# The last mixer of a two-block fp32 transformer on one core: gate and upper projection in halves, the first item's softmax beside them, a convolution of three steps a tick at the end

## What is computed

```python
u = h @ w_in
q, kc, vc, ks, vs, kw, vw, gt, cf = jnp.split(u, offs, axis=-1)
# queries and keys are normalised and rotated; 8 heads of 64, 2 groups of keys
kc = rms_norm(compress_blocks(kc_tok, cmp_pos[0], cmp_w1[0], cmp_w2[0]), k_norm[2])
vc = compress_blocks(v_cmp, cmp_pos[1], cmp_w1[1], cmp_w2[1])   # gelu(flat @ w1) @ w2
# per head: compressed attention, attention to selected blocks, attention in a window
out = gate0 * o_cmp + gate1 * o_slc + gate2 * o_win
a, b = jnp.split(cf, 2, axis=-1)
z = a * jax.nn.sigmoid(b)
z = causal_dwconv(z, conf_dw) + conf_dw_b                       # 32 taps
z = jax.nn.silu(layer_norm_2(z, conf_ln_g, conf_ln_b))
return jnp.concatenate([o_nsa, z], axis=-1) @ w_out
```

## Time and profile before

| | |
|---|---|
| Median of three runs | 2248.85 us |
| The profiled execution | 2248.29 us |
| Its span in the profile | 2246.5 us |
| PE busy | 2219.8 us, 99% of the span |
| DVE, ACT, POOL busy | 1629.2, 1196.7, 126.6 us |
| Mean granted clock of PE | 0.998 of full speed |
| DMA, mean over the span | 182 GB/s |

### The profile page before, as it was taken

How to read it: one execution, slowest core, us unless ns; L and a number is a source line. 1 busy time by engine, 2 the same in 40 slices (tenths; PEclk the granted TensorE clock), 3 DMA queues, 4 the chain that set the end, 5 groups by cost and what they waited for, 6 DMA issues and landing times.

```text
span 2246.5 us, 34599 instructions
## 1 busy us (share of the span) xinstructions
PE 2219.8 (99%) x14127; PEld 1906.0 (85%) x14127; DVE 1629.2 (73%) x2508; ACT 1196.7 (53%) x1896; POOL 126.6 (6%) x185
## 2 busy tenths in 40 slices
PE   8999999999999999999999999999999999989999
PEld 7888899878888888888898778888888888867887
DVE  5777768868676876768668777676877678666776
ACT  5555446645555545555356544555444655556653
POOL 2100010120000000000100110000000000420000
PEclk9999999999999999999999999999999999999999
DMA  7765564445556556656554446555655655643654
GB/s 237 226 190 195 189 218 123 139 153 188 191 187 193 187 185 210 191 189 196 194 180 141 135 155 210 192 186 174 206 173 173 212 188 189 199 132 117 198 176 150
DMA packets 284207, 408.17 MB, mean 182 GB/s; under 512 B 13828, under 2 KB 171072, under 8 KB 283792
## 3 DMA queue, kind: packets, MB, share of 16 engines
q1 hardware_dynamic: 276096, 380.84, 52.6%
q0 software_dynamic: 7808, 25.04, 3.7%
q10 hardware_dynamic: 144, 0.07, 0.0%
HBM read 403.98 MB, written 1.91 MB: 181 GB/s over the span
## 4 chain that ended last, share of the span: by engine, by line
PE 90%; DVE 6%; ACT 3%; DMA 1%; issue 1%; POOL 0%; SPq 0%; DVEq 0%; ACTq 0%
PE PS L575 24%; PE PS L506 12%; PE PS L513 12%; PE PS L507 12%; PE PS L574 11%; PE PS L472 2%; PE PS L473 2%; PE PS L474 2%; PE PS L577 2%; DVE WL L1391 1%; PE PS L558 1%; PE PS L557 1%; PE PS L556 1%; PE PS L492 1%; DVE QX L1698 1%
## 5 line engine op out<-in xcount | busy, mean ns | idle before, releaser
L1391 DVE TENSOR_TENSOR WL<-RW,WH 128x1024 fp32r<-128x1024 f32 (+2 forms) x678 | 803.9, 1219 | 173.2 <-ACT WH L1007 169.3
L575 PE MATMUL PS<-XT,WH 128*128 128x512 f32 x2368 | 808.0, 394 | 0.0
L1007 ACT ACTIVATE WH<-RW 128x1024 fp32r<-128x1024 f32 (+2 forms) x678 | 679.5, 1042 | 188.8 <-DMA RW<-in_w_in 39.8
L574 PE MATMUL PS<-XT,WL 128*128 128x256 f32 x2072 | 581.2, 280 | 0.0
L575 PEld LDWEIGHTS PS<-XT,WH 128*128 128x128 f32 x2368 | 425.4, 188 | 75.8
L574 PEld LDWEIGHTS PS<-XT,WL 128*128 128x128 f32 x2072 | 389.9, 188 | 13.4
L506 PE MATMUL PS<-WH,XT 128*128 128x512 f32 (+2 forms) x592 | 229.8, 392 | 1.3 <-DVE WL L1391 0.8
L507 PE MATMUL PS<-WL,XT 128*128 128x512 f32 (+2 forms) x592 | 222.2, 379 | 0.0
L506 PE MATMUL PS<-WH,HTH 128*128 128x512 f32 x488 | 192.8, 395 | 0.0
L507 PE MATMUL PS<-WL,HTH 128*128 128x512 f32 x488 | 191.6, 393 | 0.0
L513 PE MATMUL PS<-WH,XT 128*128 128x512 f32 (+2 forms) x592 | 174.1, 380 | 0.0
(11 more groups left out here) (519 smaller groups left out, 3281.6 us busy)
## 6 DMA issues: line engine op xcount, KB each, us to landing
RW<-in_w_ff_in SPq DMA_DIRECT2D x252, 512.0 KB, 4.4
RW<-in_w_ff_out SPq DMA_DIRECT2D x128, 512.0 KB, 4.3
RW<-in_w_in SPq DMA_DIRECT2D x56, 512.0 KB, 4.6
RW<-in_w_gate SPq DMA_DIRECT2D x48, 512.0 KB, 4.0
RW<-in_ffn_gate SPq DMA_DIRECT2D x44, 512.0 KB, 4.4
RW<-in_ffn_up SPq DMA_DIRECT2D x44, 512.0 KB, 4.4
RW<-in_ffn_down SPq DMA_DIRECT2D x44, 512.0 KB, 4.5
RW<-in_w_out SPq DMA_DIRECT2D x16, 512.0 KB, 5.2
```

The lines of the kernel that those rows point to most:

```text
L574: self.e.matmul(k.PS[:, b.n, 0:T], wl, k.XTH[:, kt, :], start=False, stop=False)
L575: ins = self.e.matmul(k.PS[:, b.n, :], wh, k.XT[:, kt, :], start=kt == 0, stop=kt == 7)
L1007: self.e.activation(u.hi_out, raw, ACT.Copy).then_inc(*self.s["hi"].up(u.n))
L1391: self.e.tensor_tensor(u.lo_out, raw, u.hi_out.bitcast(F), ALU.subtract).then_inc(*self.s["lo"].up(u.n))
```

## The change

It does five things.

- The keys' rotation for t = 0 is issued after the fourth step of the queries' rows and that for t = 1, with the doubled copy of the keys, after the eighth; before, both stood ahead of these rows. The two turns of paired rows move from the seventh and eighth step to the sixth and seventh.
- The gate is projected in two halves (columns 1816 and 2072 on), and so the walk is gate half 0, upper half 0, then in the tick loop gate half 1 and upper half 1. The loads of this stretch were four units of 512 KB and eight of 256 KB, and are sixteen of 256 KB: the same bytes.
- The list `beside` has eight places with the same kinds of work, and now item 0's scores behind the sixth step, its maximum behind the seventh (in one call with the compressed keys' norm and the eviction of gate half 0), and its exponentials and scale after the eighth. Item 0 has four more yields ahead of its product with the values, and each item one yield less between exponentials and scale and one at its end.
- The four copies of the compressed values (`cmp_values`, VCB) come after the norm of the compressed keys.
- From the sixteenth tick on the convolution has three steps a tick in place of two.

In the changed file the lines of `cmp_out` and after have moved by four (L1391 is L1395, L1636 is L1640, L2088 is L2092, L2112 is L2116).

```diff
@@ -1298,17 +1298,21 @@
     def cmp_out(self, b):
         k = self.k
         self.wait_ge("mm", b.full)
-        self.wait_ge("odd_g", "vcb0")
-        for i in range(4):
-            r = slice(32 * i, 32 * i + 32)
-            self.e.activation(k.VCB[r, i], k.PS[r, b.n, 128:256].rearrange("p (g d) -> p g d", g=2),
-                              ACT.Copy).then_inc(*self.s["odd_a"].up(("vcb", i)))
         kr = k.PS[:, b.n, 0:128].rearrange("p (g d) -> p g d", g=2)
         ms = k.MS[:, 24:26]
         self.e.activation(k.KCN[:, :, 0, :], kr, ACT.Square).then_inc(*self.s["odd_a"].up("ksq"))
         self.wait_ge("odd_v", "ksum")
         self.wait_ge("const_v", "eps")
         self.e.activation(ms, ms, ACT.Sqrt, bias=k.eps[1e-6], scale=1.0 / 64).then_inc(*self.s["odd_a"].up("kroot"))
+
+    def cmp_values(self, b):
+        k = self.k
+        self.wait_ge("odd_v", "kn0")
+        self.wait_ge("odd_g", "vcb0")
+        for i in range(4):
+            r = slice(32 * i, 32 * i + 32)
+            self.e.activation(k.VCB[r, i], k.PS[r, b.n, 128:256].rearrange("p (g d) -> p g d", g=2),
+                              ACT.Copy).then_inc(*self.s["odd_a"].up(("vcb", i)))
 
     def cmp_keys(self, b):
         k = self.k
...
-        for t in range(2):
-            e.rotate("k", t, 8, 12)
         e.windows()
         for _ in range(2):
             load_w1()
-        e.keys_double()
+
+        def rotated_keys(t):
+            e.rotate("k", t, 8, 12)
+            if t:
+                e.keys_double()
...
+        compressed_out = []
+
         def compressed_rows():
             b = self.bank()
             e.cmp_out(b)
             e.cmp_norm(b)
             e.prepare(ACT.Tanh)
-            self.drop(b, ("odd_a", "ksq"), ("odd_v", "kn0"))
+            compressed_out.append(b)
...
         bks = [self.bank(), self.bank()]
-        beside = [e.nothing] * 6 + [lambda: paired(0), lambda: paired(1)]
+        beside = [e.nothing, e.nothing, e.nothing, lambda: rotated_keys(0), e.nothing, lambda: paired(0),
+                  lambda: paired(1), lambda: rotated_keys(1)]
         for _ in self.rows(w, 8, 0, [(0, 512, bks)], self.x):
...
-        bks = [self.bank() for _ in range(4)]
-        beside = [lambda: e.rotate("q", 0, 0, 8), lambda: e.rotate("q", 1, 0, 8), hidden,
-                  lambda: (e.clear_vcb(), features("k", 0), features("k", 1)), hidden_turn, lambda: features("q", 0),
-                  compressed_rows, e.nothing]
-        for _ in self.cols(w, 1816, 4, bks, self.x, steps=2):
-            beside.pop(0)()
-        features("q", 1)
-        compressed_keys()
-        for j in range(4):
-            e.odd_gate(j, bks[j])
-            self.drop(bks[j], ("odd_a", ("sg", j)))
-        for n in range(2):
-            e.conv_weights(n)
-
         turned, done = set(), {0: [], 1: []}
-        later = {"q1": False}
-
-        def compressed():
-            bks = [self.bank(), self.bank()]
-            e.cmp_scores(bks)
-            for b in bks:
-                self.drop(b, ("odd_v", "cs"))
-            yield
-            yield
-            e.cmp_probs()
-            yield
-            while not later["q1"]:
-                yield
-            b = self.bank()
-            e.cmp_probs_turn(b)
-            self.drop(b, ("odd_a", "ptc"))
-            yield
...
         def item(n, t, hs):
 
-            while any(ROOM[m] == ROOM[n] and m not in turned for m in range(n)) or ROOM[n] and not later["q1"]:
+            while any(ROOM[m] == ROOM[n] and m not in turned for m in range(n)) :
                 yield
...
                 self.drop(bb[i], ("att_a", (A.id, "exp")))
             if n == 7:
                 e.prepare(ACT.Sqrt)
+            e.odd_scale(I)
             yield
-            e.odd_scale(I)
             yield
             while n >= 2 and ("out", n - 2) not in turned:
...
             yield
             yield
+            if n == 0:
+                yield
+                yield
+                yield
+                yield
             b = self.bank()
             e.odd_out(I, b)
             turned.add(("out", n))
...
+            yield
+
+        items = [item(n, t, hs) for n, (t, hs) in enumerate(
+            [(0, [0, 2]), (0, [4, 6]), (0, [1, 3]), (0, [5, 7]), (1, [0, 1]), (1, [2, 3]), (1, [4, 5]), (1, [6, 7])])]
+
+        gates, ups = [self.bank(), self.bank()], [self.bank(), self.bank()]
+
+        def gated(half, bks):
+            for j in range(2):
+                e.odd_gate(2 * half + j, bks[j])
+                self.drop(bks[j], ("odd_a", ("sg", 2 * half + j)))
+
+        def raised(half, bks):
+            for j in range(2):
+                e.odd_up(2 * half + j, bks[j])
+                self.drop(bks[j], ("odd_v", ("zc", 2 * half + j)))
+            e.conv_out(half)
+            e.conv_shift(half)
+
+        def cleared():
+            e.clear_vcb()
+            for n in range(2):
+                e.conv_weights(n)
+            features("k", 0)
+            features("k", 1)
+
+        beside = [lambda: e.rotate("q", 0, 0, 8), lambda: e.rotate("q", 1, 0, 8), hidden, cleared,
+                  lambda: (hidden_turn(), features("q", 0)), lambda: next(items[0]),
+                  lambda: (compressed_rows(), gated(0, gates), next(items[0])), e.nothing]
+        for c0, bks in ((1816, gates), (1304, ups)):
+            for _ in self.cols(w, c0, 2, bks, self.x):
+                beside.pop(0)()
+        next(items[0])
+        raised(0, ups)
+        features("q", 1)
+        compressed_keys()
+        e.cmp_values(*compressed_out)
+        self.drop(*compressed_out, ("odd_a", ("vcb", 3)), ("odd_v", "kn0"))
...
+        def compressed():
+            bks = [self.bank(), self.bank()]
+            e.cmp_scores(bks)
+            for b in bks:
+                self.drop(b, ("odd_v", "cs"))
+            yield
+            yield
+            e.cmp_probs()
+            yield
+            yield
+            b = self.bank()
+            e.cmp_probs_turn(b)
+            self.drop(b, ("odd_a", "ptc"))
             yield
...
         def upper():
 
-            for half in range(2):
+            for c0, end in ((1816 + 256, gated), (1304 + 256, raised)):
                 bks = [self.bank(), self.bank()]
-                for n, _ in enumerate(self.cols(w, 1304 + 256 * half, 2, bks, self.x)):
+                for n, _ in enumerate(self.cols(w, c0, 2, bks, self.x)):
                     if n == 3:
-                        for j in range(2):
-                            e.odd_up(2 * half + j, bks[j])
-                            self.drop(bks[j], ("odd_v", ("zc", 2 * half + j)))
-                        e.conv_out(half)
-                        e.conv_shift(half)
+                        end(1, bks)
                     yield
 
         y = self.out_odd(Operand(k.OTH, k.OTL, lambda kt, t: done[t] if kt < 4 else [("turn_lo", ("conf", t))]))
-        items = [item(n, t, hs) for n, (t, hs) in enumerate(
-            [(0, [0, 2]), (0, [4, 6]), (0, [1, 3]), (0, [5, 7]), (1, [0, 1]), (1, [2, 3]), (1, [4, 5]), (1, [6, 7])])]
-        gens = [(1, items[0]), (1, compressed()), (2, items[1]), (2, items[2]), (3, items[3]), (3, items[4]), (3, items[5]),
+        gens = [(0, items[0]), (1, compressed()), (0, items[1]), (2, items[2]), (3, items[3]), (3, items[4]), (3, items[5]),
                 (3, items[6]), (3, items[7])]
...
             ticks += 1
-            if ticks == 4:
-                later["q1"] = True
             live = [g for g in live if next(g, self) is not self]
             if up:
                 if next(up, self) is self:
                     up = None
             elif conv:
-                for _ in range(2):
+                for _ in range(2 if ticks < 16 else 3):
                     if conv and next(conv, self) is self:
                         conv = None
                         live += [conformer(0), conformer(1)]
```

More of the change, by code:

```diff
@@ L459 @@
     conv_out = conv_shift = conv_weights = conv_taps4 = conv_sum = paired = odd_q = cmp_hidden = cmp_turn = cmp_out = features = keys_double = nothing
-    cmp_norm = cmp_keys = cmp_scores = cmp_probs = cmp_probs_turn = odd_scores = odd_max = odd_scale = odd_turn = odd_out = nothing
+    cmp_norm = cmp_values = cmp_keys = cmp_scores = cmp_probs = cmp_probs_turn = odd_scores = odd_max = odd_scale = odd_turn = odd_out = nothing
     conf_turn = conf_norm = conf_back = nothing
```

## The result

The changed kernel takes 2251.49 us (median of 20 runs, 2247.76 to 2254.35), the kernel before 2247.85 (median of 20, 2245.26 to 2253.01). The ratio is 1.0016 with a 95% interval of 1.0010 to 1.0023: it is slower by 3.6 us, less than the 4.5 us that the prediction called a difference, but outside of the interval and not the 0.0 that was forecast. The profiled execution took 2249.53 us with a span of 2247.7; 16 of the 20 runs were slower than it, so the trace shows the change in one of its faster executions.

A forecast was written before the change was run, and what follows sets the result against it. TensorE bounds the kernel, busy 2219.8 of 2246.5 us, with 11.7 us of idle and low clock to win. Transposes 6.2 earlier, +3.65 late wait, +1.7 and +0.85 clock sum to 0.0: 2248.8 us, range 2244.5 to 2251.9.

The forecast's parts named there:

- (a): Keys rotated later: PE's wait before the first gate step goes from 1.53 us to 0, hidden layer begins 2.1 earlier.
- (b): Gate and upper weights loaded as sixteen units of 256 KB: same bytes, four loads more, priced at 0.
- Rival C: Narrow weight units land late and column steps wait: 6.6 us slower, 2255.4 us; chance 0.07.
- (c): First softmax, waits before L897, the second gate half and L943: 2.8 us in place of 1.38 + 2.15.
- (d): Compressed probabilities: waits before L920 and the second item's L943, taken 1.5 us; before, 1.87 before L920.
- (e): Convolution at three steps a tick: idle of the second stretch taken 1.2 us, in place of 2.50.
- (f): Last item's split stands behind the conformer on ACT and DVE: new PE wait in the output projection, +3.65 us.
- (g): Low clock behind new idles: +1.7 us behind the late wait, +0.85 (0 or 1.7) behind the item's wait.
- Rival B: The late wait before the output projection's second-half rows is hidden, the split being ready in time: 2243.5 us; chance 0.14.
- D: Clock falls at all three stalls (item 0, compressed probabilities, the end): +2.55, 2251.4 us; chance 0.13.

The follow-up runs named there:

- step ahead: Split run plus one more column step of gate half 1 ahead of the first item's turn, against the kernel before: 2241.18 us, ratio 0.9973.
- split run: Changed kernel with the last item's output split directly after its product, ahead of the conformer's activation; against the kernel before: 2246.52 us, ratio 0.9988.
- loads moved: Changed kernel with POOL's loads of the second half of Z behind its third group of diagonal copies; against the kernel before: 2248.77 us, ratio 0.9997.
- best version: Changed kernel with last split first, POOL's Z loads later and one column step ahead of the first item's turn; against the kernel before: 2239.80 us, ratio 0.9964.

## Why the prediction was wrong, step by step

- **(a), (b)** held in the changed kernel's profile. The first gate step doesn't wait, the hidden layer is 2.1 us earlier, and PE waits for no weight unit whose load is late. In three of the edited kernels, whose order is the same up to there, that step waited 0.26 to 0.63 for its cast, so the 1.53 isn't always won whole. Rival C is refuted: the kernel got slower by another mechanism. The figure of the Trainium skill ("DMA: Bandwidth & Descriptors", "Anatomy of one DMA") beside rival C is for DMAs that GpSimd issues, and these are SP's; the 2.7 us of the trace agree with it all the same.
- **(c)** held, a little too high: 0.25 + 0.33 + 1.85 = 2.4 us, 2.8 taken, at the three places named.
- **(d)** was too high: 1.5 taken, 0.1 measured. With the low clock behind item 0 one could say that slow matmuls hid it, but in the runs with the step ahead, whose low clock is 3.4 us, it was 0.33 at most as well. The chain of the compressed probabilities has more cover than I gave it.
- **(e) failed, and this is the first of the two steps that made the forecast wrong.** Taken 1.2, measured 2.0 in the profile of the changed kernel and 3.75 in that of the split run, with a fall of the clock besides. Without the meeting it is 0.4 + 0.7 = 1.1, so the propagation along the queues was right. What it lacked is that an instruction's duration, read where no POOL operation lay beside it, isn't its duration beside POOL. I wrote that POOL's copies would be the first to run short; PE never waited for one in this profile, DVE did. Price: 2.7 us in the changed kernel by the medians with the loads moved.
- **(f)** held: 3.61 for 3.65. **Its clock in (g)** was mis-sized: taken 3.4 us at half, 1.7; measured 6.8 us, some 2.7 by the instructions' starts in the profile; in two edited kernels it was 3.4 us. Medians put the whole place at 5.0 and 5.4, against 3.65 + 1.7 = 5.35 predicted.
- **(g) for item 0 failed in size, the second step.** The forecast gave back 2.1 for the old low clock and took 0.85, a mean of 0 and 1.7, for the new one: 1.25 us won. The 1.85 us stall was followed by 10.2 us of low clock, in others of the runs by 6.8 or 3.4 behind the same stall. Against the 6.8 us of the earlier trace rows it cost 1.5 more: 1.5 us lost. That is 2.75 off. (By the busy times above the old low clock had cost nearer 2.9 than 2.1; as the difference alone counts, that changes nothing here.)
- **The sum.** Forecast 0.0, found +3.6: +2.7 from the meeting, which is in no term, +2.75 from item 0's low clock, -1.8 from (c) and (d), which were taken too high, and nearly nothing from the rest. The parts come from medians and from single profiles, so that they meet 3.6 this well is in part luck. Rival B is refuted (the late wait was there). D's 2251.4 is nearest, by luck: it has no meeting, and it prices a fall behind the compressed probabilities, where no stall was left. The changed kernel's profiled execution is 2 us faster than its median; that the meeting was shorter in it than in most (PE's wait of 1.60; five profiles of other kernels with the eight copies at this place have 1.53 to 3.36) is likely, but no slower execution of this kernel was profiled.
- **Slips that decide nothing.** The low end of the range is worked out as 2244.5 and used as 2244.0; rival C's 7.0 + 0.6 + 0.68 is 8.3 and not 8.2.

What stays open is what sets the length and the beginning of a low clock. The same stall of 1.86 us in the same order was followed by 10.2, 6.8 and 3.4 us in different executions; the longer ones began 0.7 to 1.5 us after the turn of item 0, the one of 3.4 us began 3.4 us after it.

## What to carry to other kernels

Moving one group of work ahead of another in a program that is written once for all engines also moves it on queues where nobody looks: follow the last user of each queue to the end of the stage. When two engines can block each other, a duration from a trace holds only for the neighbours it had there; look which of the other engine's rows will lie beside it after the move. The length of such a meeting, and that of a low clock, differed between profiles of the same order: compare several of them before you trust one. The spread of the runs alone doesn't tell of a meeting: the twenty of the kernel before, whose product took 0.22 in its profile, spread over 7.8 us.

## What the runs showed of the hardware

- A DVE product of 128x4 took 0.16 to 0.18 us alone, 0.22 to 0.35 beside the end of a run of four or eight POOL operations, and 0.70, 1.06, 1.32, 2.72 and 2.74 beside a run of eight that began from 0.2 us after it to 1.3 us before it; POOL's eight took 3.8 instead of 2.9 where DVE got in between.
- The granted clock fell to 0.50 for 3.4, 6.8 or 10.2 us, in all thirteen profiles one of these lengths but for a fall that the end of the program cuts short. It did so behind idles of 1.85 to 3.65 us, and not behind those of 1.53 to 1.67; but also where the idles just before were 0.25, 0.33 and 0.49 only (best version). It stayed low for 10.2 us although PE was busy all the while. The Trainium skill ("TensorE: Matmul & The Clock Gate", section "Why this matters for your kernels") tells authors to leave no long idle gap between bursts of matmuls; falls behind idles agree with that in kind, but those behind 1.85 to 2.28 us come at shorter gaps than it names, and the one of the best version comes without a long gap.
